# The delta rule's triangular inverses in blocks of 64, eight heads to a tile, two blocks in opposite quarters of the array

## The chip, the cores and the metric

One core of one Trainium2 chip runs the whole kernel. The time is device microseconds of one execution, and a measurement is the median of several.

## The reference

Two transformer blocks on 256 tokens of width 1024, in float32. Most of the work is products with weights (a dense feed-forward network, eight experts, a second block with three kinds of attention). The part that the change touches is the gated delta rule of the first block: 8 heads of 128, tokens in chunks of 64:

```python
a = jnp.einsum('bhnid,bhnjd->bhnij', k_beta, k) * decay
a = jnp.where(strict, a, 0.0) + jnp.eye(c, dtype=a.dtype)
u = lax.linalg.triangular_solve(a, v_beta, left_side=True, lower=True, unit_diagonal=True)
w = lax.linalg.triangular_solve(a, k_beta * jnp.exp(gc)[..., None],
                                left_side=True, lower=True, unit_diagonal=True)
...
v_new = u_c - jnp.einsum('bhck,bhkv->bhcv', w_c, state)
o = (jnp.einsum('bhck,bhkv->bhcv', q_c * jnp.exp(gc_c)[..., None], state)
     + jnp.einsum('bhij,bhjv->bhiv', qk_c, v_new))
```

The kernel does the same in chunks of 128 tokens: for each of 2 chunks and 8 heads it needs the inverse of a unit triangular matrix of 128 x 128.

## The kernel before

**Engines and buffers.** Each engine has its own hand-written program; semaphores order them. TensorE (`pe`) writes small results to four PSUM banks in turn (`tp_bank`): batch b waits until batch b-4 was read by its owner, ScalarE ("A", by `keep`) or VectorE ("D"). `result` waits until a named batch was read. An engine's instructions run in the order written, so a wait holds back all that stands behind it.

**Stages of `deltanet`.** The input projections come first, then the delta rule, then the output projection. During the delta rule no weights are split: `state["limit"]` stops that on ScalarE and VectorE, because the second chunk's buffers lie in the space of `w_lo`.

**Buffers of the rule.** `buf[name, tt, hg]` is a tile of 128 x 4 x 128 for token tile `tt` (2) and head group `hg` (2 groups of 4 heads): dec (decay, later the masked coupling of one level), A (the strictly triangular matrix, transposed), T and TT (the inverse so far and its transpose), X (an intermediate product), qk.

**Front of the rule.** For each `tt` TensorE makes decay, and for each `hg` kk, beta and qk: batches of four products (`small_products`, L583). VectorE turns them into dec, A, qk, TT and the first level's dec (L2017 to L2031, L2011); `inv_first` tells TensorE, which transposes TT (L707), with four idle products between the groups (`keep_busy`, L548) whose result nobody reads. ScalarE copies the transposed tile to T.

**Levels.** The inverse is built by doubling the size of the solved blocks: LEVELS is 1, 2, 4, ..., 64. The level of size 1 needs no product. For each of the other six, `level` masks A into dec (the part that couples neighbouring blocks), and then, for all four (tt, hg):

```python
result(("T", tt, hg) if l == 1 else ("inv_T", tt, hg, l - 1))
small_products(("X", tt, hg, l), "A", ...)        # dec^T T, ScalarE copies it to X
...
small_products(("inv_T", tt, hg, l), "D", ...)    # TT^T X, VectorE subtracts it from T (L2044)
small_products(("inv_TT", tt, hg, l), "D", ...)   # X^T TT, subtracted from TT (L2045)
```

The last level leaves inv_T out. All products are float32 of 128 x 128 by 128 columns.

**Behind the levels.** For each `tt`: the right-hand side (VectorE, `rhs_done`, into A), vnew (TensorE: TT with A), o and, for the first `tt`, the state for the second (kdec lies in T). The second `tt` needs the state of the first.

**Constants.** `cst` holds the masks, seven for the levels (`shape_constants`), and is loaded by SyncE near the start (L1216), ahead of `narrow`; TensorE waits for `setup` before its first product with the pooling matrices.

## Time and profile before

| what | value |
|---|---|
| median of 3 runs | 1978.5 us (1976.02 to 1980.71) |
| the profiled execution's own time | 1978.78 us |
| its span, first to last instruction | 1976.9 us |
| granted clock of TensorE, mean | 0.993 of 2.4 GHz |
| TensorE busy | 1923.0 us, 97% of the span |
| VectorE, ScalarE, GpSimd busy | 1475.9, 1233.5, 72.3 us |

An engine's busy time counts instructions that overlap once. PE is TensorE's matmuls and PEld its weight loads, which run beside the matmuls. Each float32 product counts as two matmuls and two weight loads ("x8" is a batch of four products). "Idle before" is the idle time of the engine just ahead of an instruction, and the arrow names what ended it.

### The profile page before, as it was taken

How to read it: one execution, taken by the hardware profiler on the slowest of the kernel's cores; microseconds unless marked ns; L12 is line 12 of the kernel's file. 1: busy time of each engine (PE TensorE's matmuls, PEld its weight loads, DVE VectorE, ACT ScalarE, POOL GpSimd, SP SyncE). 2: the span in 40 equal slices, each digit the busy share in tenths (PEclk: the TensorE clock that was granted, in tenths of full speed). 3: DMA queues.
4: the chain of work that ended last, by engine and by line, in shares of the span. 5: the costliest groups of instructions: out<-in, count | busy, mean ns of one | idle time of the engine just before them, and what ended most of it. 6: DMA issues, size and time to landing. Idle time of an engine off the chain costs nothing.

```text
span 1976.9 us, 25976 instructions
## 1 busy us (share of the span) xinstructions
PE 1923.0 (97%) x9360; PEld 1595.1 (81%) x9360; DVE 1475.9 (75%) x1297; ACT 1233.5 (62%) x1084; POOL 72.3 (4%) x107
## 2 busy tenths in 40 slices
PE   7999999898999999999999999999999999999999
PEld 6888877796788888888888888888877787788887
DVE  5654656677689898888889889898998656676554
ACT  5544566422477777878777777777767457645442
POOL 0000001000100000000000000000310200000000
PEclk9999999998999999999999999999999999999999
DMA  7974634000399999999999999999995433245552
GB/s 307 366 281 149 226 114 167 1 1 32 140 410 370 375 399 366 400 361 385 393 352 411 360 395 369 376 398 371 371 388 223 157 128 107 86 157 205 184 181 82
DMA packets 76634, 521.28 MB, mean 264 GB/s; under 512 B 8208, under 2 KB 8464, under 8 KB 17296
## 3 DMA queue, kind: packets, MB, share of 16 engines
q1 hardware_dynamic: 72224, 503.50, 66.0%
q0 software_dynamic: 4192, 16.25, 2.1%
q8 instruction: 49, 0.80, 0.2%
q10 hardware_dynamic: 144, 0.52, 0.1%
q14 instruction: 25, 0.20, 0.0%
HBM read 501.37 MB, written 18.87 MB: 263 GB/s over the span
## 4 chain that ended last, share of the span: by engine, by line
PE 74%; DVE 6%; ACT 3%; issue 2%; POOL 1%; DVEq 0%; ACTq 0%; POOLq 0%
PE bank L826 15%; PE bank L821 15%; PE bank L822 15%; PE bank L510 7%; PE bank L527 7%; PE bank L511 7%; PE bank L583 3%; PE bank L843 1%; ACT w_hi L1292 1%; DVE w_lo L2207 1%; DVE w_lo L1869 1%; DVE kT L1949 0%; PE bank L661 0%; POOL small L1764 0%; DVE xT L1900 0%
## 5 line engine op out<-in xcount | busy, mean ns | idle before, releaser
L2207 DVE TENSOR_TENSOR w_lo<-raw,w_hi 128x2048 fp32r<-128x2048 f32 x336 | 762.1, 2289 | 105.8 <-ACT w_hi L1466 101.9
L1466 ACT ACTIVATE w_hi<-raw 128x2048 fp32r<-128x2048 f32 x336 | 643.2, 1919 | 146.2 <-PE bank L826 146.0
L1869 DVE TENSOR_TENSOR w_lo<-raw,w_hi 128x2048 fp32r<-128x2048 f32 (+2 forms) x136 | 297.7, 2198 | 161.7 <-ACT w_hi L1292 160.6
L821 PE MATMUL bank<-w_hi,xT 128*128 128x512 f32 x896 | 353.7, 395 | 0.0
L1292 ACT ACTIVATE w_hi<-raw 128x2048 fp32r<-128x2048 f32 (+2 forms) x136 | 249.2, 1839 | 166.6 <-PE bank L527 159.3
L822 PE MATMUL bank<-w_hi,xT 128*128 128x512 f32 x896 | 349.2, 390 | 0.0
L510 PE MATMUL bank<-w_hi,xT 128*128 128x512 f32 (+1 forms) x784 | 309.3, 396 | 18.4 <-DVE xT L2541 8.2
L511 PE MATMUL bank<-w_hi,xT 128*128 128x512 f32 (+1 forms) x784 | 303.7, 389 | 0.0
L826 PE MATMUL bank<-w_lo,xT 128*128 128x512 f32 x896 | 240.2, 390 | 0.8 <-DVE w_lo L2207 0.7
L826 PEld LDWEIGHTS bank<-w_lo,xT 128*128 128x128 f32 x896 | 167.9, 188 | 37.3 <-DVE w_lo L2207 2.1
L822 PEld LDWEIGHTS bank<-w_hi,xT 128*128 128x128 f32 x896 | 168.4, 188 | 33.8
L821 PEld LDWEIGHTS bank<-w_hi,xT 128*128 128x128 f32 x896 | 168.3, 188 | 33.8
L527 PE MATMUL bank<-w_lo,xT 128*128 128x512 f32 (+1 forms) x784 | 192.9, 388 | 0.0
L510 PEld LDWEIGHTS bank<-w_hi,xT 128*128 128x128 f32 x784 | 149.2, 190 | 49.3 <-issue 12.1
L821 PE MATMUL bank<-w_hi,hid 128*128 128x512 f32 x448 | 176.4, 394 | 0.0
L822 PE MATMUL bank<-w_hi,hid 128*128 128x512 f32 x448 | 174.4, 389 | 0.0
L511 PEld LDWEIGHTS bank<-w_hi,xT 128*128 128x128 f32 x784 | 149.2, 190 | 28.8 <-issue 0.2
L527 PEld LDWEIGHTS bank<-w_lo,xT 128*128 128x128 f32 x784 | 144.9, 188 | 29.7
L826 PE MATMUL bank<-w_lo,hid 128*128 128x512 f32 x448 | 119.9, 389 | 0.1
L826 PEld LDWEIGHTS bank<-w_lo,hid 128*128 128x128 f32 x448 | 84.0, 188 | 18.0 <-DVE w_lo L2207 0.6
L821 PEld LDWEIGHTS bank<-w_hi,hid 128*128 128x128 f32 x448 | 84.1, 188 | 17.2 <-issue 0.2
L822 PEld LDWEIGHTS bank<-w_hi,hid 128*128 128x128 f32 x448 | 84.2, 188 | 17.2 <-issue 0.2
(425 smaller groups left out, 1934.7 us busy)
## 6 DMA issues: line engine op xcount, KB each, us to landing
raw<-in_experts_dram SPq DMA_DIRECT2D x336, 1024.0 KB, 6.9
raw<-in_tiles_dram SPq DMA_DIRECT2D x125, 1024.0 KB, 4.8
rows_in<-zeros POOLq DMA_DIRECT2D x1, 6144.0 KB, 32.4
rows_out<-zeros POOLq DMA_DIRECT2D x1, 5632.0 KB, 55.2
raw<-in_tiles_dram SPq DMA_DIRECT2D x9, 512.0 KB, 3.4
item_rows<-rows_in SPq DMA_DIRECT2D x7, 512.0 KB, 7.4
rows_out<-y_s SPq DMA_DIRECT2D x7, 512.0 KB, 3.4
row<-in_rows_dram SPq DMA_DIRECT2D x1, 1040.0 KB, 14.8
```

What stands on the lines that cost most here:

```text
L510: nc.tensor.matmul(o, x1, b1, start=j == 0 and k == 0, stop=False)
L511: nc.tensor.matmul(o, x2, b1, start=False, stop=False)
L527: last = nc.tensor.matmul(banks[tt][:, 0:n], x1, b2, start=False, stop=j == len(tiles) - 1 and k == kc - 1)
L583: last = nc.tensor.matmul(o, l, r, start=True, stop=True)
L821: nc.tensor.matmul(out, a1, b1, start=begin and k == 0, stop=False)
L822: nc.tensor.matmul(out, a2, b1, start=False, stop=False)
L826: last = nc.tensor.matmul(out, a1, w_lo[:, s, k * CB:k * CB + CB], start=False, stop=end and k == KC - 1)
L843: last = nc.tensor.transpose(b[:, k * P:k * P + P], hnat[:, f % 2, k * P:k * P + P], ident)
L1292: nc.scalar.activation(w_hi[:, i % SPL, 0:kc * w], raw[:, i % DENSE, 0:kc * w], ACT.Copy)\
L1466: nc.scalar.activation(w_hi[:, w_slot(j), :], raw[:, raw_slot(j), :], ACT.Copy).then_inc(m_hi, 1)
L1869: nc.vector.tensor_tensor(w_lo[:, i % SPL, 0:kc * w], raw[:, i % DENSE, 0:kc * w], w_hi[:, i % SPL, 0:kc * w], ALU.subtract).then_inc(spli ...
L2207: nc.vector.tensor_tensor(w_lo[:, s, :], raw[:, raw_slot(j), :], w_hi[:, s, :], ALU.subtract).then_inc(m_lo, 1)
```

## The change

**What it does.** The inverse of the 128 x 128 matrix is made from its two diagonal blocks of 64, which the levels 1 to 32 solve, and one product for the block that couples them; level 64 is gone. One tile of 128 x 8 x 64 (`blk`) now holds, for all eight heads, the first diagonal block in partitions 0 to 63 and the second in 64 to 127. Each 64 x 64 x 64 product reads and writes its own half of the partitions, so that the two blocks of a head use opposite quarters of TensorE's array (`block_products`). A batch is 16 such products in one bank, in place of two batches of four products of 128. T is now made from TT by a product with `ident2` and not by a transpose, and this stands in the first level's loop, behind the whole front; `keep_busy(4)` is gone. "X far" and "far" (8 products each per tt) make the coupling block, with minus from ScalarE, which also copies the second block of TT beside it. vnew is now two products a head: 64 rows by 64 columns for the upper tokens, 128 rows by 64 columns for the lower. On VectorE the diagonal blocks and the coupling block of A are written by three instructions of 64 partitions in place of one of 128, and the other steps of the levels handle eight heads at once. kdec has buffers of its own. The level masks shrink from 896 to 384 columns, and `ident2` adds 64.

```diff
-LEVELS = (1, 2, 4, 8, 16, 32, 64)
+LEVELS = (1, 2, 4, 8, 16, 32)
+HALF = P // 2
+HALVES = (slice(0, HALF), slice(HALF, P))
...
-                    for hg in range(2):
-                        if hg:
-                            keep_busy(4)
-                        pe.wait_ge(inv_first, 2 * tt + hg + 1)
-                        b = tp_bank(("T", tt, hg), "A")
-                        for k in range(4):
-                            last = nc.tensor.transpose(b[:, k * P:k * P + P], buf["TT", tt, hg][:, k, :], ident)
-                        last.then_inc(tp_done, 1)
+                def block_products(name, owner, left, right):
+                    b = tp_bank(name, owner)
+                    for hh in range(HEADS):
+                        for r in HALVES:
+                            last = nc.tensor.matmul(b[r, hh * HALF:hh * HALF + HALF], left[r, hh, :], right[r, hh, :],
+                                                    start=True, stop=True)
+                    last.then_inc(tp_done, 1)
...
+                    for tt in range(NT):
+                        if l == 1:
+                            pe.wait_ge(inv_first, tt + 1)
+                            b = tp_bank(("T", tt), "A")
+                            for hh in range(HEADS):
+                                for r in HALVES:
+                                    last = nc.tensor.matmul(b[r, hh * HALF:hh * HALF + HALF], blk["TT", tt][r, hh, :],
+                                                            C("ident2")[r, :], start=True, stop=True)
+                            last.then_inc(tp_done, 1)
+                        pe.wait_ge(inv_level, (l - 1) * NT + tt + 1)
+                        result(("T", tt) if l == 1 else ("inv_T", tt, l - 1))
+                        block_products(("X", tt, l), "A", blk["dec", tt], blk["T", tt])
+                    for tt in range(NT):
+                        result(("X", tt, l))
+                        if l > 1:
+                            result(("inv_TT", tt, l - 1))
+                        block_products(("inv_T", tt, l), "D", blk["TT", tt], blk["X", tt])
+                        block_products(("inv_TT", tt, l), "D", blk["X", tt], blk["TT", tt])
+                up, low = HALVES
+                for tt in range(NT):
+                    result(("inv_T", tt, len(LEVELS) - 1))
...
+                        last = nc.tensor.matmul(b[low, hh * HALF:hh * HALF + HALF], blk["A far", tt][up, hh, :],
+                                                blk["T", tt][up, hh, :], start=True, stop=True)
...
+                    result(("X far", tt))
+                    result(("inv_TT", tt, len(LEVELS) - 1))
...
+                        last = nc.tensor.matmul(b[up, hh * HALF:hh * HALF + HALF], blk["X", tt][low, hh, :],
+                                                blk["TT", tt][low, hh, :], start=True, stop=True)
...
+                            nc.tensor.matmul(b[up, cols], blk["TT", tt][up, hh, :], x[up, k, :], start=True, stop=True)
+                            last = nc.tensor.matmul(b[low, cols], blk["far", tt][:, hh, :], x[:, k, :], start=True,
+                                                    stop=True)
...
+                for tt in range(NT):
+                    keep_blocks(("X far", tt), blk["X", tt], low)
+                for tt in range(NT):
+                    result(("inv_TT", tt, len(LEVELS) - 1))
+                    own(nc.scalar.activation(blk["far", tt][low, :, :], blk["TT", tt][low, :, :], ACT.Copy))
+                    keep_blocks(("far", tt), blk["far", tt], up, scale=-1.0)
...
-                        tell(nc.vector.tensor_tensor(a, bank4(("beta", tt, hg)), a, ALU.mult), tp_free["D"])
+                        for r in HALVES:
+                            own(nc.vector.tensor_tensor(blk["A", tt][r, now, :], beta[r, :, r], a[r, :, r], ALU.mult))
+                        tell(nc.vector.tensor_tensor(blk["A far", tt][up, now, :], beta[up, :, low], a[up, :, low],
+                                                     ALU.mult), tp_free["D"])
...
+                        for name, x in (("inv_T", blk["T", tt]), ("inv_TT", blk["TT", tt])):
+                            b = batch((name, tt, l))[:, :].rearrange("p (h c) -> p h c", c=HALF)
+                            tell(nc.vector.tensor_tensor(x, x, b, ALU.subtract), tp_free["D"])
+                            if name == "inv_T" and l < len(LEVELS) - 1:
+                                level(l + 1, tt)
```

**TensorE, one level, before.** The numbers behind the names tell the buffers apart: 72 to 83 are the first head group and 84 to 95 the second, even numbers the first token tile.

```order
L583 MATMUL bank<-T_76,dec_72 128x128 x4
L583 MATMUL bank<-T_88,dec_84 128x128 x4
L583 MATMUL bank<-T_77,dec_73 128x128 x4
L583 MATMUL bank<-T_89,dec_85 128x128 x4
L583 MATMUL bank<-X_80,TT_78 128x128 x4
L583 MATMUL bank<-TT_78,X_80 128x128 x4
L583 MATMUL bank<-X_92,TT_90 128x128 x4
L583 MATMUL bank<-TT_90,X_92 128x128 x4
L583 MATMUL bank<-X_81,TT_79 128x128 x4
L583 MATMUL bank<-TT_79,X_81 128x128 x4
L583 MATMUL bank<-X_93,TT_91 128x128 x4
L583 MATMUL bank<-TT_91,X_93 128x128 x4
```

**The same level now.** Half as many batches, each of 16 products of 64 rows and 64 columns (here and below a row names the size of the result).

```order
L721 MATMUL bank<-T_76,dec_72 64x64 x16
L721 MATMUL bank<-T_77,dec_73 64x64 x16
L721 MATMUL bank<-X_80,TT_78 64x64 x16
L721 MATMUL bank<-TT_78,X_80 64x64 x16
L721 MATMUL bank<-X_81,TT_79 64x64 x16
L721 MATMUL bank<-TT_79,X_81 64x64 x16
```

What moved: both head groups of a token tile are in one batch, and six batches stand where twelve did.

**VectorE in the front of the rule, one head group, before.**

```order
L2023 TENSOR_TENSOR dec_72<-dec_72,cst 128x512
L2025 TENSOR_TENSOR A_74<-bank,dec_72 128x512
L2026 TENSOR_TENSOR A_74<-bank,A_74 128x512
L2027 TENSOR_TENSOR qk_82<-bank,dec_72 128x512
L2030 TENSOR_TENSOR TT_78<-A_74,cst 128x512
L2031 TENSOR_TENSOR TT_78<-cst,TT_78 128x512
L2011 TENSOR_TENSOR dec_72<-A_74,cst 128x512
```

**The same place now, the second head group and what follows it.** T_88 is where A's diagonal blocks lie, TT_90 holds the coupling block.

```order
L2079 TENSOR_TENSOR dec_84<-dec_84,cst 128x512
L2081 TENSOR_TENSOR A_86<-bank,dec_84 128x512
L2085 TENSOR_TENSOR T_88<-bank,A_86 64x256 x2
L2086 TENSOR_TENSOR TT_90<-bank,A_86 64x256
L2088 TENSOR_TENSOR qk_94<-bank,dec_84 128x512
L2091 TENSOR_TENSOR TT_78<-T_88,cst 128x512
L2092 TENSOR_TENSOR TT_78<-cst,TT_78 128x512
L2066 TENSOR_TENSOR dec_72<-T_88,cst 128x512
```

What moved: the product with beta went from one instruction to three narrower ones, and the last three rows come once for both head groups.

**TensorE from the start of the last level to vnew, before.**

```order
L583 MATMUL bank<-T_76,dec_72 128x128 x4
L583 MATMUL bank<-T_88,dec_84 128x128 x4
L583 MATMUL bank<-T_77,dec_73 128x128 x4
L583 MATMUL bank<-T_89,dec_85 128x128 x4
L583 MATMUL bank<-TT_78,X_80 128x128 x4
L583 MATMUL bank<-TT_90,X_92 128x128 x4
L583 MATMUL bank<-TT_79,X_81 128x128 x4
L583 MATMUL bank<-TT_91,X_93 128x128 x4
L583 MATMUL bank<-A_74,TT_78 128x128 x4
L583 MATMUL bank<-A_86,TT_90 128x128 x4
```

**The same place now, with the first four products of vnew.**

```order
L751 MATMUL bank<-T_76,TT_90 64x64 x8
L751 MATMUL bank<-T_77,TT_91 64x64 x8
L759 MATMUL bank<-TT_78,X_80 64x64 x8
L759 MATMUL bank<-TT_79,X_81 64x64 x8
L777 MATMUL bank<-A_74,TT_78 64x128
L778 MATMUL bank<-A_74,dec_84 64x128
L777 MATMUL bank<-A_74,TT_78 64x128
L778 MATMUL bank<-A_74,dec_84 64x128
```

What moved: eight batches of four products became four batches of eight smaller ones, and vnew changes between two shapes of product from one row to the next, 8 times in each batch of 4 heads.

## Rows read from the trace of the kernel before

**Rows 1.** The page, part 1: busy time and share of each engine

```profile
PE 1923.0 (97%) x9360; PEld 1595.1 (81%) x9360; DVE 1475.9 (75%) x1297; ACT 1233.5 (62%) x1084; POOL 72.3 (4%) x107
```

**Rows 2.** Busy time by stretch of the delta rule, us from the span's start

```profile
core 0: us, PE busy (x) PEld busy (x) DVE busy (x) ACT busy (x) POOL busy (x), PEclk, DMA share, GB/s
...
379.20:392.70 13.50, 11.91 (x83) 9.46 (x82) 11.94 (x19) 2.46 (x4) 0.00 (x0) 1.00 0.00 0
392.70:403.40 10.70, 10.70 (x98) 10.70 (x97) 5.73 (x9) 2.98 (x5) 0.00 (x0) 1.00 0.01 2
...
425.40:436.50 11.10, 11.05 (x99) 10.87 (x99) 8.34 (x13) 2.39 (x4) 0.00 (x0) 1.00 0.01 2
...
447.50:456.80 9.30, 7.70 (x67) 7.31 (x65) 6.26 (x11) 2.39 (x4) 0.00 (x0) 1.00 0.01 2
456.80:459.15 2.35, 2.04 (x15) 1.85 (x16) 2.07 (x3) 0.60 (x1) 0.00 (x0) 1.00 0.00 0
466.90:471.50 4.60, 2.83 (x16) 2.64 (x17) 4.43 (x6) 0.60 (x1) 0.00 (x0) 0.81 0.01 4
```

**Rows 3.** Timeline of one level: start, us, engine, line, operation, xcount [idle before]

```profile
425.57 4.05 PE L583 MATMUL bank<-T,dec 128*128 128x128 f32 x32
...
426.72 0.60 ACT L1360 ACTIVATE X<-bank 128x512 f32<-128x512 f32 x1 [7.44 <-PE bank L583]
426.99 0.69 DVE L2045 TENSOR_TENSOR TT<-TT,bank 128x512 f32<-128x512 f32 x1
...
427.71 0.69 DVE L2011 TENSOR_TENSOR dec<-A,cst 128x512 f32<-128x512 f32 x1
428.46 0.97 PEld L583 LDWEIGHTS bank<-T,dec 128*128 128x128 f32 x8 [0.23 <-DVE dec L2011]
...
429.35 0.97 PEld L583 LDWEIGHTS bank<-X,TT 128*128 128x128 f32 x8
...
430.62 0.69 DVE L2044 TENSOR_TENSOR T<-T,bank 128x512 f32<-128x512 f32 x1 [2.21 <-PE bank L583]
```

**Rows 4.** Weight loads of L583 and of L661: ns min/median/max, times, forms

```profile
L583 PEld LDWEIGHTS bank<-T,dec x192: 186/192/192, 392.7 to 451.3; 128*128 128x128 f32 x192
...
L661 PEld LDWEIGHTS bank<-squares,cst x32: 93/97/151, 319.0 to 327.1; 128*16 128x16 f32 x32
```

**Rows 5.** Timeline of products that stream 8 columns past 128 columns of weights

```profile
529.67 0.30 PEld L779 LDWEIGHTS bank<-rt,cst 128*128 128x128 f32 x2
...
529.89 0.30 PEld L780 LDWEIGHTS bank<-rt,cst 128*128 128x128 f32 x2
```

**Rows 6.** Timeline of weight loads where the rows in use change, and where not

```profile
1647.56 0.29 PEld L971 LDWEIGHTS bank<-k_foxT,q_foxT 64*128 64x128 f32 x2
1647.97 0.30 PEld L972 LDWEIGHTS bank<-cst,small 128*128 128x128 f32 x2
...
1649.23 0.30 PEld L975 LDWEIGHTS bank<-cst,small 128*128 128x128 f32 x2
1649.45 0.30 PEld L976 LDWEIGHTS bank<-cst,small 128*128 128x128 f32 x2
```

**Rows 7.** One DVE line at two widths: ns min/median/max, times, forms

```profile
L2585 DVE TENSOR_TENSOR hid<-bank,hid x12: 425/692/693, 86.8 to 216.1; 128x512 fp32r<-128x512 f32 x10, 128x256 fp32r<-128x256 f32 x2
```

**Rows 8.** Granted clock (the number behind POOL's) by stretch

```profile
466.00:469.70 3.70, 1.73 (x14) 1.35 (x12) 3.53 (x6) 0.60 (x1) 0.00 (x0) 1.00 0.00 0
469.80:473.00 3.20, 3.17 (x15) 3.18 (x16) 2.44 (x2) 0.60 (x1) 0.00 (x0) 0.50 0.02 5
...
323.10:327.30 4.20, 4.20 (x21) 1.88 (x20) 4.16 (x7) 2.72 (x6) 0.00 (x0) 1.00 0.70 246
```

**Rows 9.** The constants' load, its rate (second slice), TensorE's wait near the start

```profile
GB/s 307 366 281 149 226 114 167 1 1 32 140 410 370 375 399 366 400 361 385 393 352 411 360 395 369 376 398 371 371 388 223 157 128 107 86 157 205 184 181 82
...
cst<-in_consts_dram SPq DMA_DIRECT2D x1, 943.5 KB, 15.9
...
28.29 0.45 PE L1115 MATMUL bank<-pool_m,pool_u 128*128 128x256 f32 x1 [1.54 <-DMA narrow<-in_narrow_dram]
```

More of the change, by code:

```diff
@@ L87, in shape_constants @@
     put("iota", np.broadcast_to(j, (P, P)))
-    put("levels", np.concatenate([(i // (2 * s) == j // (2 * s)) & (i // s % 2 == 0) & (j // s % 2 == 1)
+    r, c2 = i % HALF, np.arange(HALF)[None, :]
+    put("ident2", r == c2)
+    put("levels", np.concatenate([(r // (2 * s) == c2 // (2 * s)) & (r // s % 2 == 0) & (c2 // s % 2 == 1)
                                   for s in LEVELS], axis=1))
@@ L249, in build @@
                                                          offset=low_parts + 2048 * (6 * _h + _i))
+        kdec = [buf["dec", 0, 0], buf["T", 0, 1]]
+        blk = {}
+        for _tt in range(NT):
+            for _n, _home in (("dec", ("dec", 0)), ("far", ("dec", 1)), ("T", ("T", 0)), ("A", ("T", 1)),
+                              ("TT", ("TT", 0)), ("A far", ("TT", 1)), ("X", ("X", 0))):
+                blk[_n, _tt] = buf[_home[0], _tt, _home[1]][:, :, :].rearrange("p a b -> p (a b)")\
+                    .rearrange("p (h c) -> p h c", c=HALF)
         hidden1 = hid1[:, :, :].rearrange("p a b -> p (a b)")
@@ new lines, in deltanet @@
+                up, low = HALVES
+                for tt in range(NT):
+                    result(("inv_T", tt, len(LEVELS) - 1))
+                    b = tp_bank(("X far", tt), "A")
+                    for hh in range(HEADS):
+                        last = nc.tensor.matmul(b[low, hh * HALF:hh * HALF + HALF], blk["A far", tt][up, hh, :],
+                                                blk["T", tt][up, hh, :], start=True, stop=True)
+                    last.then_inc(tp_done, 1)
+                for tt in range(NT):
+                    result(("X far", tt))
+                    result(("inv_TT", tt, len(LEVELS) - 1))
+                    b = tp_bank(("far", tt), "A")
+                    for hh in range(HEADS):
+                        last = nc.tensor.matmul(b[up, hh * HALF:hh * HALF + HALF], blk["X", tt][low, hh, :],
+                                                blk["TT", tt][low, hh, :], start=True, stop=True)
+                    last.then_inc(tp_done, 1)
@@ L735, in deltanet @@
                         pe.wait_ge(rhs_done, 2 * tt + hg + 1)
-                        result(("inv_TT", tt, hg, len(LEVELS) - 1))
-                        small_products(("vnew", tt, hg), "A", lambda b: [
-                            (o, buf["TT", tt, hg][:, k, :], buf["A", tt, hg][:, k, :]) for k, o in enumerate(four(b))])
+                        result(("far", tt))
+                        b = tp_bank(("vnew", tt, hg), "A")
+                        for k, hh in enumerate(heads(hg)):
+                            x, cols = buf["A", tt, hg], slice(k * P, k * P + P)
+                            nc.tensor.matmul(b[up, cols], blk["TT", tt][up, hh, :], x[up, k, :], start=True, stop=True)
+                            last = nc.tensor.matmul(b[low, cols], blk["far", tt][:, hh, :], x[:, k, :], start=True,
+                                                    stop=True)
+                        last.then_inc(tp_done, 1)
                     for hg in range(2):
@@ L745, in deltanet @@
                             small_products(("state", 0, hg), "A", lambda b: [
-                                (o, buf["T", tt, hg][:, k, :], buf["X", tt, hg][:, k, :]) for k, o in enumerate(four(b))])
+                                (o, kdec[hg][:, k, :], buf["X", tt, hg][:, k, :]) for k, o in enumerate(four(b))])
                 keep_busy(10)
@@ L2007, in by_head, with of_level, level @@
                     return m.unsqueeze(1).broadcast_to((P, 4, P))
-                def level(l, tt, hg):
-                    tell(nc.vector.tensor_tensor(buf["dec", tt, hg][:, :, :], buf["A", tt, hg][:, :, :],
-                                                 by_head(C("levels")[:, l * P:l * P + P]), ALU.mult), inv_level)
+                def of_level(l):
+                    return C("levels")[:, l * HALF:l * HALF + HALF].unsqueeze(1).broadcast_to((P, HEADS, HALF))
+                def level(l, tt):
+                    tell(nc.vector.tensor_tensor(blk["dec", tt], blk["A", tt], of_level(l), ALU.mult), inv_level)
+                up, low = HALVES
                 for tt in range(NT):
```

47 lines of the change are left out of this document (17 added, 30 removed).

## The prediction

> **What bounds the kernel now.** I read the page first: TensorE is busy for 1923 us, 97% of the span [rows 1], so nearly everything that shortens it elsewhere changes nothing. Then I cut the delta rule into stretches. The reader is to see in [rows 2] that from 392.7 to 447.5 us TensorE is busy without a break (11.05 of 11.10 us in one level), VectorE for 8.34, ScalarE for 2.39, and that DMA moves nothing: no weights are fetched or split here, so what the rule loses or gains goes into the end one to one. Ahead of it, from 379.2 to 392.7, VectorE sets the pace (11.94 of 13.50). The levels are therefore bound by TensorE's 12 batches of four products, 0.89 us each: in [rows 3] two loads that begin batches one behind the other start at 428.46 and 429.35.
>
> The timeline [rows 3] also gives the distances that a shorter batch would lay bare. A batch begins to load at 429.35 and VectorE reads it at 430.62: 1.27 us, 0.89 of batch and 0.38 of latency. ScalarE's copy is 0.60. VectorE's step is 0.69 and the next follows 0.03 later (426.99 to 427.71), so 0.72. VectorE is done at 428.40 and TensorE goes on at 428.46, so 0.06.
>
> **The change, part by part.** Everything hangs on the time p of a batch of 16 quarter products, 32 passes of load and matmul. A pass takes 0.112 us now (0.89 for 8). A load of 16 columns is 95 ns shorter than one of 128 [rows 4], 0.85 ns a column, so 64 columns save 54 ns. Shortening only the streamed side would give nothing: products with 8 streamed columns and 128 columns of weights still start 0.22 us apart, as now [rows 5]. Here both sides are halved, so a pass should take 0.056 to 0.058. One after the other, 32 passes make p = 1.79, exactly the two batches that they replace. If the two quarters work side by side, p is 0.90. No row shows two quarters at work; these are the bounds. I take 0.96, near the lower one, because the two products of a head share no row or column of the array, with a little for starts.
>
> *Front.* For each token tile VectorE did 16 steps of 0.72 and two narrow ones of 0.46, 12.4 us. Now there are 2 of 0.72 and 2 of 0.46 for the decay, 3 of 0.72 and 3 narrow ones for each head group, and 3 of 0.72 for the tile. A step of 256 columns takes 425 ns where one of 512 takes 692 [rows 7], 0.455 with its gap: 11.6 us. That is 0.85 less, twice. The transposes no longer stand on TensorE between the two tiles' products, and VectorE's wait there (part of the 1.56 us that it is idle in the second stretch of the front [rows 2]) goes, 1.0. Together **-2.7**.
>
> *Level 1*, counted from the moment when VectorE has signalled the last TT. Before: four transposes, 0.4, and then 392.7 to 403.4 [rows 2], together 11.1 us. Now T of the second tile takes p, latency, copy and restart 1.04, then X and four batches follow: 6p + 1.04 = 6.8 at p = 0.96. **-4.3**.
>
> *Levels 2 to 5.* Before 44.1 us (403.4 to 447.5) [rows 2]. Now a level is the longer of 6p (5.8) and the loop through VectorE: X of the second tile waits for the fifth VectorE step behind the first tile's T (T, dec, TT, T, dec), so 2p + 0.38 + 5 x 0.72 + 0.06 = 5.96. VectorE, today hidden with 2.7 us to spare, becomes the bound, barely. Four levels 23.8. **-20.3**.
>
> *Last level against the coupling block.* Before 9.3 us from 447.5 to 456.8. Now both X far use one quarter only, so nothing overlaps: 16 passes, 0.90 each. With the copy (1.04) far begins at 1.94 and ends at 2.84, and ScalarE must copy a block of TT before it copies far: ready at 4.1. **-5.2**.
>
> *vnew.* Each head's two products use 64 and then 128 rows. [rows 6]: a product of 64 rows and the one of 128 behind it start 0.41 apart, products of one shape 0.22. So a change of rows costs 0.19 us, of which 0.11 is a load of 128 columns that no longer runs beside a matmul; for 64 columns I count 0.06 + 0.09. A product is then 0.36, a batch 2.9 us in place of 0.89. First tile: 5.8 against 2.35, +3.4. Second tile: the second batch waits for VectorE until 2.9 us behind the first anyway 466.9 to 471.5 in [rows 2], so the first is hidden and the second costs 2.9 against 1.7: +1.2. **+4.6**; the bounds are 1.1 (a change costs nothing, only the 16 passes of 128 columns count) and 5.9 (0.41 for each).
>
> *Clock.* [rows 8]: after a stretch in which TensorE was busy for 1.73 of 3.70 us the granted clock was 0.50, that is 1.2 GHz, in the next 3.2 us. The idle products are gone, and TensorE now waits at the end of the front for VectorE and then for the copy of T, with about as small a share of work. I count one such fall more, which costs half of its length: **+1.7**. Bounds -1.7 (the fall at 469.8 goes instead) and +3.4 (two).
>
> *Constants.* 448 of 1887 columns are no longer loaded, 224 KB, 0.6 us at 366 GB/s [rows 9], and TensorE waits 1.54 us for the last load behind them. **-0.6**, bounds 0 and -1.5.
>
> Sum: -2.7 - 4.3 - 20.3 - 5.2 + 4.6 + 1.7 - 0.6 = -26.8. From the profiled execution's 1978.8 us this gives **1952**; the median of the runs is 0.3 lower, which changes nothing.
>
> **Rules of the skill.** The Trainium skill (TensorE: Matmul & The Clock Gate, Part 3) says that a weight load passes matmuls in flight if its row group differs, and that matmuls in different parts of the array start about 4 ns apart; by that p would be at its lower bound, and no run here shows it. The Trainium skill (TensorEngine Tiling (Array Packing), Restrictions and Gotchas) says the contrary for this layout: different row tiles are to write to different PSUM banks and cannot access one bank at the same time. Both quarters of a batch write one bank; by that rule the serial case below would come, 1976.
>
> **The rivals.**
> *Serial quarters.* The two products of a head run one behind the other, for instance since both write one bank, or since weight loads queue. Then p = 1.79, level 1 takes 11.8 (+0.7), the four levels 43.0 (-1.1), and the sum is -2.6: **1976**. For it: TensorE's load side alone fills every pass today (0.22 for 8 columns), and the trace has no two loads at once. Against: only that the quarters are disjoint.
> *Partial overlap.* p of 1.35 gives -2.0 and -11.7 for the levels, **1963**.
> *A stop at each change of quarter* (slower). If going from one quarter to the other costs what a change from 64 to 128 rows costs, 0.15 us for a product, p is 4.1, and 30 batches take 69 us more than serial: **2045**. It decides from p = 2.0 on, 14 ns more for a product than serial. For it: every change of the rows in use in [rows 6] costs. Against: there the number of rows changes, here only which.
> *Low clock.* Quarters leave part of the array idle; were the clock 1.2 GHz throughout, overlap would be lost again: about 1979. Against: from 323.1 to 327.3 the clock was full while products used 16 of 128 columns [rows 4, 8].
>
> **How the numbers follow.** Overlap 0.50, partial 0.12, serial 0.20, low clock 0.04, stop at each change 0.14. A measurement of this kernel tells 0.2%, 4 us, from no change. The overlap case ranges over its own bounds from 1944 to 1956; the range must take in serial (with vnew and clock at their upper bounds 1979) and leaves out the slow case: 1946 to 1981. Faster by over 0.2%: overlap, partial and a little of serial, 0.65; within 0.2%: 0.21; slower 0.14.
>
> **What would show it.** In the profile after: batches of quarter products about 0.96 us apart and levels of 6.0 (serial: 1.8 and 10.7); VectorE's steps one behind the other in a level; 4.1 us from the last level to vnew; products of vnew 0.36 apart; one stretch at 0.50 near the end of the front; a shorter wait near 28 us. The prediction is wrong if p is over 1.2, if vnew changes shape free of charge, or if the clock falls within the levels.

## The result and the profile after

Over four executions each the changed kernel takes 1947.16 us (1946.42 to 1951.39) and the kernel before 1978.59 us; the ratio is 0.9846, with a 95% interval from 0.9828 to 0.9864. The profiled execution took 1951.39 us with a span of 1949.6, so the two traces are 27.3 us of span apart. The forecast was 1952 us and 26.8 us less.

The page of the kernel after, part 1 (each engine's busy time, share of the span, instructions), beside [rows 1]:

```profile
PE 1897.9 (97%) x9904; PEld 1567.8 (80%) x9904; DVE 1448.9 (74%) x1263; ACT 1227.2 (63%) x1074; POOL 72.3 (4%) x107
```

TensorE is busy for 25.1 us less and is still the bound. The kernel after by stretches (columns as in [rows 2]): the front, level 2, the last level with the coupling block, the first tile's vnew, and the second tile's vnew with the output products behind it:

```profile
356.70:387.20 30.50, 22.82 (x224) 20.45 (x224) 21.27 (x37) 9.78 (x15) 0.00 (x0) 1.00 0.01 1
393.80:399.65 5.85, 5.84 (x200) 5.70 (x197) 4.14 (x7) 1.19 (x2) 0.00 (x0) 1.00 0.01 3
...
417.05:421.15 4.10, 3.96 (x78) 3.82 (x74) 3.71 (x6) 2.43 (x5) 0.00 (x0) 1.00 0.02 4
421.15:426.95 5.80, 5.76 (x33) 3.04 (x33) 0.00 (x0) 1.79 (x3) 0.00 (x0) 1.00 0.00 0
434.70:442.25 7.55, 7.55 (x47) 4.79 (x48) 5.69 (x7) 1.19 (x2) 0.00 (x0) 1.00 0.00 1
```

A level took 11.10 us in [rows 2] and takes 5.85. Its timeline in the kernel after (start, us, engine, line, operation, instructions, idle time before), where [rows 3] had batches 0.89 apart:

```profile
401.79 1.02 PEld L721 LDWEIGHTS bank<-X,TT 64*64 64x64 f32 x32
...
402.73 1.02 PEld L721 LDWEIGHTS bank<-TT,X 64*64 64x64 f32 x32
...
405.53 1.02 PEld L721 LDWEIGHTS bank<-T,dec 64*64 64x64 f32 x32
...
405.95 0.69 DVE L2066 TENSOR_TENSOR dec<-T,cst 128x512 f32<-128x512 f32 x1
...
406.70 1.01 PEld L721 LDWEIGHTS bank<-T,dec 64*64 64x64 f32 x32 [0.15 <-DVE dec L2066]
...
407.63 1.02 PEld L721 LDWEIGHTS bank<-X,TT 64*64 64x64 f32 x32
```

Batches of 16 quarter products are 0.93 to 0.94 apart: that is p, the time of one batch, and the quarters overlap. From 401.79 to 407.63 is one level, 5.84; its six batches need 5.6, and the second tile's X (406.70) waited for VectorE's dec, which ended at 406.64.

The first tile's vnew, timeline of the kernel after, with the products of 64 and of 128 rows 0.36 apart:

```profile
422.24 0.19 PEld L778 LDWEIGHTS bank<-A,dec 128*64 128x64 f32 x2 [0.17 <-issue]
...
422.61 0.19 PEld L777 LDWEIGHTS bank<-A,TT 64*64 64x64 f32 x2 [0.17 <-issue]
```

The last term is the clock. First the kernel before, by stretches; the number behind POOL's is the granted clock, 1.00 being 2.4 GHz and 0.50 being 1.2 GHz: a fall near 50 us, the work behind it, and the fall near 490:

```profile
48.00:54.00 6.00, 4.75 (x14) 3.79 (x15) 5.79 (x8) 2.38 (x2) 0.00 (x0) 0.72 0.73 243
54.28:84.28 30.00, 30.00 (x139) 24.89 (x138) 17.40 (x13) 16.71 (x17) 4.06 (x8) 1.00 0.93 356
...
486.50:493.00 6.50, 4.90 (x19) 3.95 (x18) 6.21 (x10) 5.68 (x9) 0.00 (x0) 0.52 0.57 213
```

And the kernel after, at the places that answer to these:

```profile
47.30:53.30 6.00, 4.72 (x21) 3.95 (x22) 5.79 (x8) 2.42 (x2) 0.00 (x0) 1.00 0.74 243
53.60:82.00 28.40, 28.40 (x132) 23.58 (x131) 17.40 (x13) 16.73 (x17) 4.06 (x8) 1.00 0.92 350
...
453.50:463.00 9.50, 8.21 (x27) 6.89 (x28) 9.14 (x12) 5.70 (x9) 0.00 (x0) 0.50 0.47 166
495.00:497.50 2.50, 2.50 (x7) 1.93 (x7) 2.23 (x9) 0.21 (x1) 0.00 (x0) 0.50 0.03 7
...
1536.00:1538.50 2.50, 2.50 (x7) 1.91 (x7) 2.50 (x2) 0.00 (x0) 0.00 (x0) 0.50 0.48 95
```

The fall near 50 is gone, and the stretch behind it is 1.6 us shorter; so is the fall of [rows 8] in the second vnew. The one behind the idle products lasts from 453.2 to 463.5, where it lasted from 486.8 to 493.7, and two are new (494.2 to 497.7 and 1535.2 to 1538.7). From the first idle product to the router's first one it is now 57.3 us (442.26 to 499.54), where it was 55.0 (474.07 to 529.11), and from there to the end of the span 1450.1 where it was 1447.8, though nothing in either was changed. The fall in the second vnew [rows 8] had cost about 1.6 us, half of the 3.2 us that it lasts in that row. So the clock's share is put at -1.6 - 1.6 + 2.2 + 2.2: it took back 1.2 us. The two 2.2 are what is left over in stretches that did not change. Ten traces bear out the second: from the router's first product to the end of the span it takes 1447.8 to 1447.9 us where no fall stands near 1535 (before, and the runs bridge, combined and best below) and 1450.0 to 1450.3 where one does (the changed kernel twice, v_grouped, v_wide, l_order, best_again). The same six have a fall between 491 and 500. The runs best and best_again are one kernel and lie on either side, so these two falls come and go between executions of one kernel. The fall near 1535 is about 3.4 us long and goes with 2.2 us of time, more than the half that the prediction counts; why isn't shown.

### The profile page after: what moved, and what is told of

Its sections match the earlier page's. It is cut to its first block, busy times and chain, and to the rows that moved or that the text cites. A ratio compares the mean times of both kernels' runs of the same rounds, so it can differ in the third digit from the quotient of the medians.

```text
span 1949.6 us, 26960 instructions
## 1 busy us (share of the span) xinstructions
PE 1897.9 (97%) x9904; PEld 1567.8 (80%) x9904; DVE 1448.9 (74%) x1263; ACT 1227.2 (63%) x1074; POOL 72.3 (4%) x107
## 4 chain that ended last, share of the span: by engine, by line
PE 75%; DVE 5%; ACT 3%; issue 2%; POOL 1%; DVEq 0%; ACTq 0%; POOLq 0%
PE bank L868 15%; PE bank L863 15%; PE bank L864 15%; PE bank L524 7%; PE bank L525 7%; PE bank L541 7%; PE bank L721 1%; PE bank L885 1%; PE bank L597 1%; ACT w_hi L1334 1%; DVE w_lo L2267 1%; DVE w_lo L1921 1%; DVE kT L2001 0%; PE bank L675 0%; POOL small L1816 0%
```

## The experiments

Ratios are to the kernel before on the same chip. Where a few microseconds are at stake the whole time says little, as will be seen, so the readings come from the traces.

### Products measured by themselves

In place of the ten idle products stand eleven groups on constants; the fourth reads

```diff
-                keep_busy(10)
...
+                for k in range(32):
+                    r = HALVES[k // 2 % 2]
+                    last = nc.tensor.matmul(o64(one, r, k), wr(r), wr(r), start=True, stop=True)
+                fence(last)
...
```

> In place of the ten idle products ahead of the output projection TensorE runs eleven groups of products on constants, each group waiting for the one before; nothing else is changed, so the kernel's time says nothing. Every product of the first eight groups is 64x64x64, two passes, 32 of them. My theory is that products overlap only when they share neither rows nor columns: one quarter alone 3.7 us for 32 (0.058 a pass), opposite quarters in turn 1.9 in one bank and 1.9 in two banks, the same quarter twice in turn 2.8 to 3.7, four times in turn 3.3 to 3.7, same columns with other rows 3.7, same rows with other columns 3.7, all four quarters in turn 1.9. First rival, by the skill's rule that a load may pass matmuls in flight if its row group differs: same columns with other rows also 1.9, same rows with other columns 3.7, all four quarters about 1.9. Second rival, bank rule: opposite quarters in one bank slower than in two. Third rival, cost goes by area: one quarter alone 1.9 too, and nothing depends on the order. Three groups of 16 products with 128 streamed columns: one quarter 1.9 to 3.6, opposite quarters in turn 0.95 to 1.8, 128 rows with the two column halves in turn 1.9 to 3.6.

Timeline of that kernel, TensorE alone, one row for each group. In order of lines: one quarter; opposite quarters in turn in one bank; the same in two banks; in twos; in fours; same columns, rows in turn; same rows, columns in turn; all four quarters in turn; then with 128 streamed columns one quarter, opposite quarters in turn, and 128 rows with the column halves in turn.

```profile
443.76 3.94 PE L807 MATMUL bank<-cst 64*64 64x64 f32 x64
447.76 2.08 PE L811 MATMUL bank<-cst 64*64 64x64 f32 x64
449.91 2.08 PE L815 MATMUL bank<-cst 64*64 64x64 f32 x64
452.06 2.13 PE L819 MATMUL bank<-cst 64*64 64x64 f32 x64
454.25 2.69 PE L823 MATMUL bank<-cst 64*64 64x64 f32 x64
456.99 2.08 PE L827 MATMUL bank<-cst 64*64 64x64 f32 x64
459.14 2.08 PE L830 MATMUL bank<-cst 64*64 64x64 f32 x64
461.29 1.16 PE L834 MATMUL bank<-cst 64*64 64x64 f32 x64
462.54 3.70 PE L837 MATMUL bank<-cst 64*64 64x128 f32 x32
466.31 1.96 PE L841 MATMUL bank<-cst 64*64 64x128 f32 x32
468.34 1.97 PE L844 MATMUL bank<-cst 128*64 128x128 f32 x32
```

Cost by area falls: one quarter takes 3.94, about 0.058 a pass with 0.2 of latency (each product is two passes of load and matmul, so a group has 64), and two in turn half of it, 0.029. My theory falls with it in its narrow form. Quarters that share their columns (L827) or their rows (L830) overlap as well as opposite ones, and all four in turn run nearly four at a time (1.16, less the same 0.2 about 15 ns a pass). So in these groups what counts is only that neighbours in the order are not the same quarter. One bank and two banks take the same where the outputs lie in opposite halves of the bank; two row halves that write the same half of one bank were not tried. The Trainium skill (TensorEngine Tiling (Array Packing), Restrictions and Gotchas) says that row tiles cannot access one bank at once; by that L811 would be slower than L815, and the trace does not agree. The Trainium skill (TensorE: Matmul & The Clock Gate, Part 3) lets a load pass matmuls if its row group differs; the trace agrees (L827, 2.08 us), and shows the same gain with the same rows too (L830, 2.08 us).

The second measurement, with longer runs of one quarter (32 products in eights, then in sixteens), vnew's two shapes in turn, 128 rows in one column half, and 600 products each:

> As in the first measurement of products by themselves, in place of the ten idle products: 32 products 64x64x64 in opposite quarters, eight of one and then eight of the other; 32 with sixteen and sixteen; 16 that stream 128 columns with 64 and 128 rows in turn, as vnew has them; 16 of 128 rows and 64 columns that stream 128, all in one column half; then 600 products in one quarter and 600 in opposite quarters in turn. The kernel's time says nothing. Theory (TensorE takes weight loads ahead of running products only over a few instructions, so a run of one quarter costs its own length beyond that): groups of eight 3.0 to 3.6 us, sixteen 3.4 to 3.8, against 2.08 in turn and 2.69 in fours. Rival (it looks ahead without bound): 2.1 for both. vnew's alternation 5.8 for 16 (0.36 each), one column half 3.7 (0.23 each). Clock: if work in one quarter counts as too little for the full clock, the granted clock falls to 0.50 in the 600 of one quarter and rises in the 600 in turn (70 us then 35 at full clock; 100 or more and 35 if it falls); if any busy TensorE holds the clock, it is 1.00 in both.

```profile
446.76 3.40 PE L808 MATMUL bank<-cst 64*64 64x64 f32 x64
450.23 3.76 PE L812 MATMUL bank<-cst 64*64 64x64 f32 x64
454.05 5.84 PE L816 MATMUL bank<-cst 64*64 64x128 f32 x32
459.95 3.71 PE L820 MATMUL bank<-cst 128*64 128x128 f32 x32
463.71 70.21 PE L825 MATMUL bank<-cst 64*64 64x64 f32 x1200
533.98 35.21 PE L829 MATMUL bank<-cst 64*64 64x64 f32 x1200
```

3.94, 3.76, 3.40 and 2.69 us with no, one, three and seven changes of quarter (the first and the last from the measurement above): each change saves 0.18, the time of three passes, until everything is paired. The overlap reached no farther in these groups. The shapes in turn cost 0.365 a product and one shape 0.23, so a change of shape is 0.13. Both long groups stayed at a clock of 1.00, 70.2 and 35.2 us: one quarter at work did not lose the full clock in 70 us.

### All of one quarter first

```diff
-                    for hh in range(HEADS):
-                        for r in HALVES:
+                    for r in HALVES:
+                        for hh in range(HEADS):
```

> Every batch issues its eight upper-quarter products first and the eight lower ones behind them; the work is the same. Theory (two quarters run side by side, and only if they are neighbours in the order): a batch takes 1.8 us in place of 0.93, a level about 10.8 in place of 5.85, the kernel some 26 us more than the changed kernel, 1972 to 1976, 0.997 of before. Rival (the cost of a product goes by its area, or the engine looks far enough ahead to pair them anyway): batches of 0.93, 1947.

Three of its four executions took 2008 to 2010 us, and one 1965.63. In the profiled one a batch takes 2.68 us; its stretches before and in the levels:

```profile
360.00:387.00 27.00, 21.54 (x200) 19.77 (x198) 20.65 (x37) 7.20 (x12) 0.00 (x0) 0.94 0.01 2
390.00:460.00 70.00, 69.98 (x835) 70.00 (x836) 16.54 (x24) 5.37 (x9) 0.00 (x0) 0.50 0.01 2
```

The order alone costs the overlap, as the theory says, but not all that it costs is overlap. The clock fell at 388.2 us, where TensorE waits for VectorE at the end of the front, and stayed at half until 487.3, through 99 us in which TensorE was nearly always busy. The levels are only the first 80 of them: it also stayed low through vnew, whose products of 64 and 128 rows run in turn from 474 to 483.7, and it was back 3.6 us after the first product on the whole array. At half clock batches in turn would take 1.87, so the order makes a batch 1.43 times as long; by 0.18 saved for each change (two a batch) it would be 1.5 us at full clock, not 1.8. The one execution of 1965.63 has no trace, but its mean granted clock was 0.993, as in the changed kernel, and 0.967 in the other three. As an estimate, 30 batches of 1.5 in place of 0.93 are 17 us more, 1964 where the changed kernel has 1947. So by this estimate the lost overlap costs some 17 us, and the low clock the other 43 or so. The low clock that I had given 4 in 100 is real, in this order.

### Does one quarter raise the clock?

The idle products are left out, TensorE waits 11.5 us for the normed output, and then come 400 products in one quarter and 400 in turn.

> The idle products are left out and TensorE waits for VectorE's normed output, some 11 us, so that the clock falls; behind that wait come 400 products in one quarter and then 400 in opposite quarters in turn. The kernel's time says nothing. Theory (work in one quarter can't raise the clock, as in the grouped kernel, whose levels ran at 0.50 from 390 us on to their end): 0.50 through all 400, about 93 us for them, and 1.00 soon after the quarters alternate, 23 us. Rival (the clock comes back after a few microseconds of any busy TensorE, and the grouped kernel was disturbed by something else): 1.00 within 5 us, 47 us for the first 400.

Timeline, and the granted clock by stretch:

```profile
457.16 85.59 PE L809 MATMUL bank<-cst 64*64 64x64 f32 x800 [11.47 <-DVE xn L2167]
542.82 24.52 PE L813 MATMUL bank<-cst 64*64 64x64 f32 x800
```

```profile
458.00:541.00 83.00, 83.00 (x781) 83.00 (x780) 1.44 (x1) 0.00 (x0) 0.00 (x0) 0.50 0.04 14
545.00:560.00 15.00, 15.00 (x519) 15.00 (x518) 0.00 (x0) 0.00 (x0) 0.00 (x0) 1.00 0.01 3
```

83 us of an always busy TensorE didn't bring the clock back, and it was back at 545.0 us, 2.2 us after the first of the alternating products. Together with the 70 us at 1.00 above: in both measurements work in one quarter kept the clock that it found. This is the likely reason why the grouped kernel stayed at 1.2 GHz once it had fallen (though its vnew, which isn't work in one quarter, did not bring the clock back either). With quarters in turn the clock also fell where the levels begin, and came back: in the first measurement kernel, whose rule is that of the changed kernel, it was low from 386.2 to 393.1, and in best_again below from 389.3 to 396.2.

### vnew's shapes

First the four products of 64 rows of a batch and then the four of 128:

```diff
                         for k, hh in enumerate(heads(hg)):
-                            nc.tensor.matmul(b[up, cols], ...)
-                            last = nc.tensor.matmul(b[low, cols], ...)
+                            nc.tensor.matmul(b[up, k * P:k * P + P], ...)
+                        for k, hh in enumerate(heads(hg)):
+                            last = nc.tensor.matmul(b[low, k * P:k * P + P], ...)
```

> Within each vnew batch the four products of 64 rows come first and the four of 128 rows behind them, so the shape changes twice and not eight times; same work. Theory (each change of the rows in use costs about 0.14 us): a batch takes 1.6 to 1.9 us in place of 2.88, three of the four batches are on the path, the kernel gains 3 to 4 us on the changed kernel, 1943 to 1944. Rival (the products themselves are slow, 0.36 each, whatever stands beside them): batches stay 2.9 and the time 1947.

Ratio 0.9844 (0.9822 to 0.9866). Timeline, TensorE:

```profile
421.39 1.05 PE L777 MATMUL bank<-A,TT 64*64 64x128 f32 x8 [0.19 <-issue]
422.37 1.09 PE L780 MATMUL bank<-A,dec 128*64 128x128 f32 x8
423.39 1.08 PE L777 MATMUL bank<-A,TT 64*64 64x128 f32 x8
```

A batch takes 2.0 and not 2.88: the changes were what made it long. It is more than the 1.6 to 1.9 that I expected: a quarter that streams 128 columns takes 0.11 a pass (3.70 us for 32 in L837, latency taken off), no less than a whole product, so 16 passes are 1.8, and the two changes of shape add 0.2. The stages give 2.6 us, the time nothing that can be told.

Then both products of a head with 128 rows, the upper block over zeros, in the two column halves:

```diff
-                            nc.tensor.matmul(b[up, cols], blk["TT", tt][up, hh, :], x[up, k, :], start=True, stop=True)
-                            last = nc.tensor.matmul(b[low, cols], blk["far", tt][:, hh, :], x[:, k, :], start=True,
-                                                    stop=True)
+                            for r, name in ((up, "up"), (low, "far")):
+                                last = nc.tensor.matmul(b[r, k * P:k * P + P], blk[name, tt][:, hh, :], x[:, k, :],
+                                                        start=True, stop=True)
...
+                    own(nc.scalar.activation(blk["up", tt][up, :, :], blk["TT", tt][up, :, :], ACT.Copy))
```

> The upper block of TT is copied by ScalarE into a tile whose lower half is zero, so each vnew product has 128 rows, and a head's two products differ in the column half alone; ScalarE zeroes two half tiles during level 2 and copies one half tile more for each token tile ahead of vnew. Theory (no change of shape, and two column halves run side by side as in the products measured by themselves, 0.061 us a pass): a vnew batch takes 0.98 in place of 2.88, vnew starts 0.6 later, first tile 0.6 - 3.8 = -3.2, second tile -1.9, together -5.1: 1942 where the changed kernel has 1947. Rival (128 rows load into both column halves one behind the other): batches of 1.9, -2.3.

Ratio 0.9841 (0.9818 to 0.9863). Timeline of the output's first product behind two such batches, which began at 422.79 (start, us, engine):

```profile
424.49 0.27 PE L778 MATMUL bank<-A,dec 128*64 128x128 f32 x1
425.32 1.16 PE L597 MATMUL bank<-X,qk 128*128 128x128 f32 x8 [0.56 <-ACT X L1402]
```

The batches take 0.89 each: two column halves do run side by side. Of the 4.0 us that this saves in the first tile (two batches of 0.89 in place of 2.88), 0.65 goes to ScalarE's extra copy, as expected, and 0.8 to a wait that I had not counted: ScalarE still makes the second tile's copies when the first vnew could be fetched. First tile -2.55, second (read where the clock was full, in the last kernel below) -1.9.

### The order of a level

```diff
                         block_products(("inv_T", tt, l), "D", blk["TT", tt], blk["X", tt])
+                    for tt in range(NT):
                         block_products(("inv_TT", tt, l), "D", blk["X", tt], blk["TT", tt])
...
-                    for tt in range(NT):
-                        for name, x in (("inv_T", blk["T", tt]), ("inv_TT", blk["TT", tt])):
+                    for name in ("inv_T", "inv_TT"):
+                        for tt in range(NT):
```

> TensorE multiplies both tiles' inv_T batches ahead of both inv_TT batches, and VectorE takes T, dec, T, dec, TT, TT in place of T, dec, TT, T, dec, TT. Theory (a level of 5.84 us is bound by the loop through VectorE, whose fifth step releases X of the second tile): X now waits for the fourth, the level comes down to TensorE's six batches and ScalarE's copy, 5.6 to 5.7, 0.6 to 1.0 us less in four levels, no wait of TensorE on VectorE's dec there. Rival (the idle 0.27 us of a level is the start of a batch and would be there anyway): 5.84 as before.

Ratio 0.9843 (0.9818 to 0.9868). Timeline, the first X,TT batch of three levels:

```profile
398.12 2.07 PE L721 MATMUL bank<-X,TT 64*64 64x64 f32 x64
...
403.75 2.07 PE L721 MATMUL bank<-X,TT 64*64 64x64 f32 x64
...
409.39 2.07 PE L721 MATMUL bank<-X,TT 64*64 64x64 f32 x64
```

5.64 a level, and no wait for dec. So VectorE's fifth step was the bound of the level, by 0.2 us. The rival is out: had the idle 0.27 us been the start of a batch, it would have stayed.

### The changed kernel again, the idle products, and all together

> The changed kernel once more, as the standard for its neighbours on this chip and as a second trace of it. Theory (the falls of the granted clock wander between executions, the stages do not): batches 0.93, levels 5.84, vnew batches 2.88 again, but falls to 0.50 at other places than in the first trace, the sum of the falls 2 to 12 us long; time 1946 to 1951. Rival (the change itself moves the fall behind the idle products to ten microseconds and adds one at the end of the rule): the falls at 453.5 to 463 and at 495 stand there again.

1950.87 us (1945.63 to 1952.97), ratio 0.9848 (0.9825 to 0.9871). From the first X of level 1 to the idle products it took 57.70 us (386.79 to 444.49), and 57.72 in the first trace (384.54 to 442.26). Some of its falls stand elsewhere:

```profile
366.00:369.10 3.10, 3.10 (x18) 3.10 (x17) 2.23 (x4) 1.79 (x2) 0.00 (x0) 0.53 0.03 8
459.00:465.00 6.00, 4.39 (x13) 3.50 (x14) 5.75 (x9) 3.81 (x5) 0.00 (x0) 0.73 0.71 262
495.00:500.00 5.00, 3.95 (x11) 3.17 (x12) 4.55 (x14) 1.30 (x2) 0.00 (x0) 0.66 0.01 3
1536.00:1540.00 4.00, 4.00 (x16) 3.29 (x15) 4.00 (x2) 0.48 (x1) 0.00 (x0) 0.62 0.28 53
```

One at the front's end is new (as are others near 28, 52 and 280 us), the one behind the idle products is a third as long, and those near 495 and 1536 are there again, so neither side is wholly right. The stages are the same to 0.02 us, as the theory says.

`keep_busy(16)` in place of `keep_busy(10)`:

> Sixteen idle products in place of ten ahead of the output projection, 2.6 us more of them, so that TensorE is busy until VectorE has the normed output (it waits 2.9 us for that now). Theory (the clock falls behind this wait, and 9.5 us at 1.2 GHz cost 4.7): no fall there, the kernel gains 2 to 5 us, 1943 to 1945. Rival (the fall comes from the light work of the idle products themselves or from the wait for the first weights, not from the 2.9 us): the fall stays, the time is 1947.

1950.06 us, ratio 0.9857 (0.9836 to 0.9877). I had taken an idle product for one pass of 0.43 us; it is two. With sixteen of them TensorE goes on 1.7 us later after the first idle load than with ten (13.4 against 11.7). The wait of 2.9 us is gone, and still the clock falls, from 461.0 to 464.5, as it did from 461.7 to 465.2 with ten in the second trace: in this trace it isn't the wait that sets the fall. From the first idle product to the router's it takes 56.7 us, as in that trace (56.6). Nothing was gained.

> v_wide, the order of l_order and the sixteen idle products in one kernel. If the three are worth 5.1, 0.8 and 2 to 5 us and don't touch each other, it takes 1937 to 1940, 0.980 of before. If the fall of the clock isn't set by the wait, 1941; if falls wander freely, a trace shows the stages shortened and the time spreads by 3 us around that.

1946.85 us, ratio 0.9845 (0.9822 to 0.9868): the stages were shortened (52.2 us from the first X to the idle products, 386.39 to 438.62, where the changed kernel has 57.7), the time was not shown to be.

The last version takes thirteen idle products and moves ScalarE's copies:

```diff
+                copy_blocks(0)
                 for tt in range(NT):
                     keep_blocks(("X far", tt), blk["X", tt], low)
...
                         keep(("vnew", tt, hg), buf["X", tt, hg][:, :, :])
+                    if tt == 0:
+                        copy_blocks(1)
```

> combined, with thirteen idle products in place of sixteen, ScalarE's two copies of the first tile's TT taken ahead of the X far copies (it is idle there), and those of the second tile behind the first tile's vnew copies. Theory (in combined vnew waited 0.9 us for ScalarE and its copy of X held the output's products up by 0.6): from the end of the last level to the output's products 5.8 us in place of 7.33 (9.89 in the changed kernel), a level 5.64, the second tile 5.7, and 13 products of 0.87 end 0.4 ahead of the normed output, so that no time is lost as in combined, where sixteen ended 1.7 behind it. By the stages 9 us less than the changed kernel, with 2 us of spread from the falls of the clock: 1938 to 1943, 0.980 to 0.982 of before. Rival (the chain runs through VectorE's right sides and not through ScalarE): 7.3 as in combined, 1942 to 1945.

1948.04 us (1942.41 to 1950.44), ratio 0.9848 (0.9835 to 0.9862).

> The same kernel as best once more, since its trace showed 5.5 us less between the first product of level 1 and the idle products, while its median (1948.0, ratio 0.9848, 0.9835 to 0.9862) was no lower than that of the changed kernel. Theory (the stages hold, and falls of the clock elsewhere, 2 to 8 us in an execution, covered them by chance): a ratio of 0.981 to 0.984 and the same stages in the trace. Rival (a shorter rule brings its own falls behind it, so that the end is where it was): a ratio of 0.9848 again, with falls of the clock after 450 us in the trace.

1948.87 us (1944.86 to 1951.92), ratio 0.9841 (0.9816 to 0.9865). In both traces the way from the end of the last level to the output's first product is 6.2 us (417.55 to 423.76 in the first; 9.9 in the changed kernel, 417.05 to 426.94; I expected 5.8), and the second tile's 5.7. All the same, the spans of the two traces are 1940.6 and 1947.1 us. The levels' beginning in the first and in the second:

```profile
387.00:394.00 7.00, 5.41 (x176) 5.30 (x178) 3.40 (x6) 1.19 (x2) 0.00 (x0) 1.00 0.01 2
```

```profile
387.00:394.00 7.00, 4.68 (x95) 4.38 (x93) 2.53 (x4) 1.65 (x3) 0.00 (x0) 0.66 0.01 2
```

In the second the clock was down there, so that the way from the first X to the idle products took 54.0 us and not 52.1, and at several more places where the first had none. So 5.5 us less in the stages, seen at full clock in two traces (combined 52.2, best 52.1), are not shown as a shorter time: the two ratios are 0.9848 and 0.9841, and the changed kernel's are 0.9846 and 0.9848.

The granted clock of each execution suggests where the 5.5 us went. Its mean is 0.9936 over the nine executions of the changed kernel and 0.9910 over the ten of the last version. Of a span of some 1946 us that is 12.5 and 17.5 us lost to the low clock, an estimate that takes a fall to cost half its length. By that estimate the last version lost 5 us more to the clock, about what its stages had saved. Whether the shorter rule brings these falls stays open: combined, whose stages are as short, has 0.9936 over its five, and best and best_again are one kernel and lost to the clock in different places. No version is shown to beat the changed kernel.

## Why the prediction was right, and where it wasn't

| term | forecast | traces | |
|---|---|---|---|
| front | -2.7 | -2.8 | 33.3 (359.0 to 392.3) against 30.5 |
| level 1 | -4.3 | -4.5 | 11.1 against 6.6 |
| levels 2 to 5 | -20.3 | -20.9 | 44.1 against 23.2 |
| last level, coupling block | -5.2 | -5.2 | 9.3 against 4.1 |
| vnew, first tile | +3.4 | +3.4 | 2.34 against 5.77 |
| vnew, second tile | +1.2 | +2.0 | both at full clock |
| clock | +1.7 | +1.2 | -1.6 -1.6 +2.2 +2.2, in part what was left over |
| constants | -0.6 | -0.7 | 28.26 against 27.58 |
| sum | -26.8 | -27.5 | span: -27.3 |

- **Overlap** was the likeliest case and came, p being 0.93 where I took 0.96. The reason that I gave, "share no row or column of the array", is too narrow: sharing one of them does no harm (L827, L830).
- **The level** became bound by the loop through VectorE, 5.84 where I had 5.96, and the new order shows that it was this loop. The 0.12 between them is worth 0.5 us of the 0.6 by which the levels were missed.
- **vnew** was right in its product (0.36) and nearly in its parts (a change of 0.13 where I had 0.15, a product of 0.23 where I had 0.22). Its lower bound should be 1.3 by its own terms (batches of 1.79 against 2.35 and 1.7), not 1.1; nothing hangs on it. The second tile was mis-sized: I set 2.9 against 1.7, but those 1.7 of [rows 2] were run at half clock, which the clock's lower bound then counted once more. At full clock it is 0.89, so that from the first product of this vnew to the idle products before would have taken 2.90 + 0.89 + 1.78 = 5.57, and after it is 7.57 (434.69 to 442.26).
- **The clock** came out near its term by luck. I put one more fall at the front's end. The first trace has none there. Eleven of the twelve later ones, in which the front is the same, do have one between 360 and 398. In the first trace the sum comes from two falls lost and others new or longer, and the one that was lost near 50 us is there again in the second trace of the same kernel.
- **Constants**: the 0.7 is luck too, or at least not shown. In the twelve other traces with the smaller load TensorE's first pooled product starts at 27.55 to 28.27 us, and once at 28.95; before, it started at 28.29. In the trace after, it no longer waits for the load of `narrow` but for ScalarE's `pool_u` (0.89 us), so the load is no longer what holds it up. One trace of before is too little to say more.
- **The rivals**: serial quarters appear only if the order puts one quarter's products in a row, partial overlap likewise (an estimated 1.5 in eights). No stop at a change of quarter: it saves 0.18. A clock that stays low came only with the grouped order and with one quarter alone, behind a fall; in both traces of the changed kernel it was full in the levels. By the Trainium skill's rule on banks (TensorEngine Tiling (Array Packing), Restrictions and Gotchas) the serial case would have come; L811 and L815 above, 2.08 us each, show that it doesn't hold for outputs in opposite halves of a bank.
- The median of 1947.2 is 4.8 below the forecast, and the profiled execution, the slowest of the four, 0.6. Single executions of this kernel lie between 1945.6 and 1953.0; the sum was made against traces, and the falls in a trace come and go by as much.

## What to carry to other kernels

Here small products cost by passes, and two or four of them ran at once when neighbours in the order lay in different parts of the array; write the loop so that the part changes innermost, and don't let the number of rows change with it. Once a stage is halved, the next bound may be close (here 5.84 against 5.6 us): count the loop through the other engines, and the copies that sit in an engine's queue ahead of the one that is waited for. Where falls of the clock move by several microseconds between executions of one kernel, judge an edit of a few microseconds by its stage in the trace, and don't promise the time.

## What the runs showed of the hardware that I had not expected

- Four quarters in turn take about 15 ns a pass, two in turn 29 (opposite ones or such as share rows or columns), one alone 58. A change of quarter saves 0.18 us, whether a run is 4, 8 or 16 products long, and twos already pair nearly as well as single ones (2.13 against 2.08).
- One quarter at work kept the full clock for 70 us but didn't bring it back in 83 us; it was back 2 us after alternating quarters began. In the grouped order three of four executions had a mean clock of 0.967 (in the trace, 0.50 for 99 us at a stretch) and took some 60 us more than the changed kernel, of which an estimated 43 are the clock's.
- Two traces of one kernel are 6.5 us apart in span (1940.6 and 1947.1), and their mean granted clocks are 0.996 and 0.989.
